# A two-block transformer kernel: the feed-forward down projections computed by one level of Strassen's scheme

## What is computed

```python
D_MODEL, SEQ, D_FF = 1024, 512, 2816
# first block
f = (jax.nn.silu(h @ ffn_w_gate[l]) * (h @ ffn_w_up[l])) @ ffn_w_down[l]
x = x + rmsnorm(f, post_ffn_norm[l])
# second block, layers 0 and 1
h = causal_dwconv_2(x @ w_up, conv_w)
g, v = jnp.split(h, 2, axis=-1)
f = (jax.nn.silu(g) * v) @ w_down
x = layer_norm(ALPHA * x + f, ln_g[layer, 1], ln_b[layer, 1])
```

## Time and profile before

| | |
|---|---|
| median of 3 runs | 1866.66 us (1864.05 to 1867.01) |
| span of the profiled execution | 1862.7 us |
| TensorE busy | 1826.8 us, 98% |
| VectorE, ScalarE, GpSimd busy | 928.4, 723.4, 342.4 us |
| down projections, first to last matmul | 553.28 to 674.50, 1208.72 to 1329.94, 1735.42 to 1854.88 us |

### The profile page before, as it was taken

How to read it: one execution, slowest core, us unless ns; L and a number is a source line. 1 busy time by engine, 2 the same in 40 slices (tenths; PEclk the granted TensorE clock), 3 DMA queues, 4 the chain that set the end, 5 groups by cost and what they waited for, 6 DMA issues and landing times.

```text
span 1862.7 us, 23259 instructions
## 1 busy us (share of the span) xinstructions
PE 1826.8 (98%) x9750; PEld 1527.4 (82%) x9750; DVE 928.4 (50%) x1455; ACT 723.4 (39%) x1221; POOL 342.4 (18%) x206
## 2 busy tenths in 40 slices
PE   7999988999999999999999999999999999999998
PEld 6788977888888888777788888888788898888886
DVE  5686644332232244785455555523574455555334
ACT  6664344322322243557634343321333243343211
POOL 1434533111110033321141111100201321111000
PEclk9999999999999999999999999999999999999999
DMA  5212032233223232110122223332332323222331
GB/s 198 74 57 69 8 125 81 91 110 119 99 100 104 87 135 92 68 46 24 46 78 103 91 91 98 118 113 80 113 103 80 112 91 109 95 91 94 122 102 68
DMA packets 29653, 171.53 MB, mean 92 GB/s; under 512 B 3378, under 2 KB 6490, under 8 KB 11754
## 3 DMA queue, kind: packets, MB, share of 16 engines
q1 hardware_dynamic: 29548, 170.03, 26.5%
HBM read 167.88 MB, written 3.68 MB: 92 GB/s over the span
## 4 chain that ended last, share of the span: by engine, by line
PE 94%; DVE 3%; ACT 1%; POOL 1%; DMA 0%; issue 0%; SPq 0%; ACTq 0%
PE ps L578 28%; PE ps L580 28%; PE ps L579 27%; PE ps L1116 2%; PE ps L1083 1%; PE ps L1079 1%; PE ps L1101 1%; POOL wL L2505 1%; PE ps L658 1%; PE ps L708 1%; PE ps L1047 1%; ACT wH L1287 1%; DVE hL L1825 1%; PE ps L862 0%; PE ps L871 0%; DMA x<-in_x 0%
## 5 line engine op out<-in xcount | busy, mean ns | idle before, releaser
L578 PE MATMUL ps<-hH,wH 128*128 128x512 f32 (+1 forms) x1568 | 594.9, 379 | 4.4 <-DVE rows L2240 1.5
L580 PE MATMUL ps<-hH,wL 128*128 128x512 f32 (+1 forms) x1568 | 590.0, 376 | 0.0
L579 PE MATMUL ps<-hL,wH 128*128 128x512 f32 (+1 forms) x1568 | 589.9, 376 | 0.0
L1818 DVE TENSOR_TENSOR wL<-raw,wH 128x1024 fp32r<-128x1024 f32 (+1 forms) x212 | 259.4, 1263 | 331.8 <-ACT wH L1287 331.8
L1287 ACT ACTIVATE wH<-raw 128x1024 fp32r<-128x1024 f32 (+2 forms) x298 | 290.3, 1023 | 273.6 <-PE ps L580 273.5
L578 PEld LDWEIGHTS ps<-hH,wH 128*128 128x128 f32 x1568 | 295.1, 188 | 59.3 <-DVE rows L2240 2.0
L580 PEld LDWEIGHTS ps<-hH,wL 128*128 128x128 f32 x1568 | 295.0, 188 | 54.3
L579 PEld LDWEIGHTS ps<-hL,wH 128*128 128x128 f32 x1568 | 295.2, 188 | 52.3
L2505 POOL TENSOR_TENSOR wL<-raw,wH 128x1024 fp32r<-128x1024 f32 (+2 forms) x86 | 205.0, 2406 | 670.2 <-ACT wH L1287 662.4
L578 PE MATMUL ps<-wH,aH 128*128 128x512 f32 x528 | 205.6, 389 | 0.0
L580 PE MATMUL ps<-wH,aL 128*128 128x512 f32 x528 | 205.4, 389 | 0.0
(11 more groups left out here) (367 smaller groups left out, 1845.5 us busy)
## 6 DMA issues: line engine op xcount, KB each, us to landing
raw<-in_wbig SPq DMA_DIRECT2D x139, 1024.0 KB, 4.8
rows<-in_rows SPq DMA_DIRECT2D x12, 512.0 KB, 6.0
x<-in_x SPq DMA_DIRECT2D x8, 512.0 KB, 5.7
raw<-in_wbig SPq DMA_DIRECT2D x8, 512.0 KB, 3.5
out<-x SPq DMA_DIRECT2D x4, 512.0 KB, 2.6
u_rows<-u_scratch SPq DMA_DIRECT2D x4, 384.0 KB
near<-u_rows SPq DMA_DIRECT2D x1, 1024.0 KB, 7.9
raw<-in_wbig SPq DMA_DIRECT2D x1, 1000.0 KB, 9.0
```

The source lines that it names most:

```text
L578: e.matmul(o, hi, m_hi, start=first, stop=False)
L579: e.matmul(o, hi, m_lo, start=False, stop=False)
L580: return e.matmul(o, lo, m_hi, start=False, stop=end)
L1818: e.tensor_tensor(wL[r][:, cs], raw[r][:, cs], wH[r][:, cs].bitcast(F32), ALU.subtract).then_inc(*low_dve.one(c, h))
```

## The change

Only the three down projections change, with what makes their inputs and takes their results. The product is cut in two along each axis: tokens (256 and 256), features (1408 and 1408, eleven k-tiles each) and columns (512 and 512). In place of eight block products there are seven, each with 11 k-tiles, two token tiles and three matmuls: 66 matmuls a product.

The core of the diff:

```diff
@@ -36,6 +36,11 @@
...
+    def blocks(name, layer):
+        plan.append((name, layer, "blocks", 11, 2048))
+        for _ in range(11):
+            plan.append((name, layer, "none", 0, 0))
...
@@ -413,12 +425,18 @@
...
         R = Region(BIG, TOP)
-        aH = R("aH", [128, 22, 512], F32R)
-        aL = R("aL", [128, 22, 512], F32R)
...
+        aR = R("aR", [128, 11, 1536])
...
+        ft = [R("ft", [128, 512]) for _ in range(4)]
+        agH = [R("agH", [128, 1024], F32R) for _ in range(2)]
+        agL = [R("agL", [128, 1024], F32R) for _ in range(2)]
+        extra0 = R("extra0", [128, 2048])
+        store0 = R("store0", [128, 512])
+        extra1 = at("extra1", FT, [128, 2048])
+        scaled_f = at("scaled_f", XRES + 16384, [128, 8, 512])
+        parts_f = at("parts_f", XRES + 32768, [128, 8, 512])
+        junk_f = aR[:, 0:4, 0:128]
+        raw_ring = [raw[1], raw[0], extra0, extra1]
...
@@ -560,7 +579,89 @@
...
+        def store(k):
+            return aR[:, k - 1, 512:1024] if k else store0[:, :]
...
+        def half_free(n, v):
+            if v < 4:
+                return dn.pe.at(n, "done", 9) if v < 2 else dn.pe.at(n, "P5", 1)
+            return dn.pe.at(n, "P4", 1) if v in (8, 9) else dn.pe.at(n, "done", 7 + v)
 
...
@@ -661,6 +762,83 @@
...
+            def down(n, turn_tile):
+                banks = {"P1": (4, 5), "P5": (2, 3), "P7": (0, 1), "P6": (6, 7), "P4": (4, 5), "P2": (6, 7), "P3": (0, 1)}
+                first = {"P1": (2, 0, "w01"), "P5": (0, 1, "w01"), "P7": (3, 2, "w2"), "P6": (1, 3, "w3")}
...
+                for q in range(11):
+                    r = (q + 1) % 2
+                    for p in ("P1", "P5", "P7", "P6") if q < 10 else ("P1", "P6", "P7", "P5"):
+                        a, b, ready = first[p]
+                        w.wait_ge(*dn.dve.at(n, "alo", q))
+                        w.wait_ge(*dn.dve.at(n, ready, q))
+                        for j in range(2):
+                            if q == 0:
+                                clear(banks[p][j])
+                            m = product(p, j, r, a, b, q == 0, q == 10)
+                            if q == 10:
+                                m.then_inc(*dn.pe.one(n, p, j))
+                    if q < 10:
+                        m.then_inc(*dn.pe.one(n, "done", q))
...
+                for v in range(4):
+                    ready_b(v)
+                    for kk in range(2):
+                        for j in range(2):
...
+                            m = part_b(v, "P4", kk, j, v == 0 and kk == 0, False)
+                    m.then_inc(*dn.pe.one(n, "done", 11 + v))
+                for j in range(2):
...
+                for v in range(6, 13):
+                    ready_b(v)
+                    for p in ("P2", "P3"):
...
+                            m = part_b(v, p, 0, j, v == 6, False)
+                    m.then_inc(*dn.pe.one(n, "done", 11 + v))
+                    if v == 9:
+                        turn_tile(2)
+                    if v == 11:
+                        turn_tile(3)
+                for j in range(2):
+                    for vs in ((13, 14), (15, 16)) if j == 0 else ((14, 15), (13, 16)):
+                        for p in ("P2", "P3"):
+                            for v in vs:
+                                ready_b(v)
+                                m = part_b(v, p, 0, j, False, v == 16)
...
@@ -1275,20 +1451,76 @@
...
+            def high_a(n, q):
+                r, src = (q + 1) % 2, raw_a(q)
+                w.wait_ge(*(dn.pe.at(n, "done", q - 2) if q > 1 else chunk_done(DOWN[n] - 2 + q)))
+                w.wait_ge(*dn.pool.at(n, "S1", q))
+                e.activation(agH[r][:, :], aR[:, q, 0:1024], ACT.Copy).then_inc(*dn.act.one(n, "ahi", q))
+                w.wait_ge(*landed_a(n, q))
+                w.wait_ge(*dn.pool.at(n, "T1", q))
+                e.activation(wH[r][:, 0:1024], src[:, 0:1024], ACT.Copy).then_inc(*dn.act.one(n, "w01", q))
+                w.wait_ge(*dn.dve.at(n, "T3", q))
+                e.activation(wH[r][:, 1024:1536], src[:, 1536:2048], ACT.Copy).then_inc(*dn.act.one(n, "w2", q))
+                w.wait_ge(*dn.pool.at(n, "T2", q))
+                e.activation(wH[r][:, 1536:2048], store(q), ACT.Copy).then_inc(*dn.act.one(n, "w3", q))
+            def high_b(n, v):
+                w.wait_ge(*half_free(n, v))
+                if v < 6:
+                    w.wait_ge(*dn.pool.at(n, "T4", B_KS[v][-1]))
+                else:
+                    w.wait_ge(*landed_b(n, B_KS[v][0]))
+                e.activation(w_view(wH, v), w_source(v), ACT.Copy).then_inc(*dn.act.one(n, "whi", v))
+                if v >= 6:
+                    w.wait_ge(*dn.pool.at(n, "S4", B_KS[v][0]))
+                e.activation(a_view(agH, v), a_source(v), ACT.Copy).then_inc(*dn.act.one(n, "bhi", v))
...
@@ -1798,18 +2025,98 @@
...
+            def third_sum(n, q):
+                src = raw_a(q)
+                w.wait_ge(*landed_a(n, q))
+                e.tensor_tensor(src[:, 1536:2048], src[:, 1536:2048], src[:, 512:1024], ALU.subtract).then_inc(*dn.dve.one(n, "T3", q))
+            def low_a(n, q):
+                r, src = (q + 1) % 2, raw_a(q)
+                w.wait_ge(*dn.act.at(n, "ahi", q))
+                e.tensor_tensor(agL[r][:, :], aR[:, q, 0:1024], agH[r][:, :].bitcast(F32), ALU.subtract).then_inc(*dn.dve.one(n, "alo", q))
+                for name, cs, part_of in (("w01", slice(0, 1024), src[:, 0:1024]), ("w2", slice(1024, 1536), src[:, 1536:2048]),
+                                          ("w3", slice(1536, 2048), store(q))):
+                    w.wait_ge(*dn.act.at(n, name, q))
+                    e.tensor_tensor(wL[r][:, cs], part_of, wH[r][:, cs].bitcast(F32), ALU.subtract).then_inc(*dn.dve.one(n, name, q))
+            def low_b(n, v):
+                w.wait_ge(*dn.act.at(n, "whi", v))
+                e.tensor_tensor(w_view(wL, v), w_source(v), w_view(wH, v).bitcast(F32), ALU.subtract).then_inc(*dn.dve.one(n, "wlo", v))
...
+            def down(n, turn_tile, add_last, finish):
+                for q in range(1, 11):
+                    if q < 10:
+                        third_sum(n, q + 1)
+                    low_a(n, q)
...
@@ -2483,13 +2832,88 @@
...
+            def branch_sums(n, c0):
+                for m in range(22):
+                    if m == 21:
+                        weight_sums(n, 0)
+                    k = m % 11
+                    w.wait_ge(*ffn.dve.at("a", c0 + m))
+                    if m < 11:
+                        e.tensor_tensor(aR[:, k, 768:1024], aR[:, k, 512:768], aR[:, k, 768:1024], ALU.subtract).then_inc(*dn.pool.one(n, "S3", k))
+                    else:
+                        w.wait_ge(*dn.pool.at(n, "S3", k))
+                        e.tensor_tensor(aR[:, k, 256:512], aR[:, k, 1280:1536], aR[:, k, 768:1024], ALU.subtract).then_inc(*dn.pool.one(n, "S2", k))
+                        w.wait_ge(*dn.pool.at(n, "S2", k))
+                        e.tensor_tensor(aR[:, k, 0:256], aR[:, k, 256:512], aR[:, k, 512:768], ALU.add).then_inc(*dn.pool.one(n, "S1", k))
+            def weight_sums(n, q):
+                src = raw_a(q)
+                w.wait_ge(*dn.dve.at(n, "T3", q))
+                if q:
+                    w.wait_ge(*dn.dve.at(n, "alo", q - 1))
+                e.tensor_tensor(store(q), src[:, 1536:2048], src[:, 0:512], ALU.add).then_inc(*dn.pool.one(n, "T2", q))
+                e.tensor_tensor(src[:, 512:1024], src[:, 512:1024], src[:, 0:512], ALU.subtract).then_inc(*dn.pool.one(n, "T1", q))
+            def fourth_sum(n, q):
+                w.wait_ge(*dn.dve.at(n, "w3", q))
+                w.wait_ge(*landed_a(n, q))
+                w.wait_ge(*dn.pool.at(n, "T2", q))
+                e.tensor_tensor(store(q), raw_a(q)[:, 1024:1536], store(q), ALU.subtract).then_inc(*dn.pool.one(n, "T4", q))
+            def low_b(n, v):
+                w.wait_ge(*dn.act.at(n, "bhi", v))
+                e.tensor_tensor(a_view(agL, v), a_source(v), a_view(agH, v).bitcast(F32), ALU.subtract).then_inc(*dn.pool.one(n, "alo", v))
+            def down(n):
+                for q in range(1, 11):
+                    weight_sums(n, q)
...
+                def outer_sum(ks):
+                    w.wait_ge(*dn.dve.at(n, "alo", ks[-1]))
+                    w.wait_ge(*dn.pool.at(n, "S1", ks[-1]))
+                    for k in ks:
+                        e.tensor_tensor(aR[:, k, 256:512], aR[:, k, 1024:1280], aR[:, k, 256:512], ALU.subtract).then_inc(*dn.pool.one(n, "S4", k))
+                def add_x(i):
+                    if n:
+                        w.wait_ge(*ffn.act.at("x", n - 1, i))
+                        w.wait_ge(*(dn.dve.at(n, "C22", i - 2) if i > 1 else dn.dve.at(n, "P5", i)))
+                        e.tensor_tensor(q8v(x[:, i, :]), q8v(x[:, i, :]), whole(parts_f, i), ALU.add).then_inc(*dn.pool.one(n, "x", i))
+                for v in range(3):
+                    low_b(n, v)
+                add_x(2)
```

(24 more changed lines are left out.)

460 lines of the change are left out of this document (340 added, 120 removed).

## The result

| | before | after |
|---|---|---|
| median | 1865.36 us (1863.99 to 1867.01, 4 runs) | 1941.95 us (1940.74 to 1947.45, 4 runs) |
| ratio, 95% interval | | 1.0419 (1.0403 to 1.0435) |
| span of the profiled execution | 1862.7 us | 1938.9 us |
| first to last matmul start, three stages | 121.2, 121.2, 119.5 us | 135.9, 147.4, 150.5 us |

The change costs 4.2%; the two medians are 76.6 us apart. The prediction was 1939.0 us. The page of after answers to the earlier trace rows: TensorE is busy for 10 us less and its share of the chain fell from 94% to 74%, with VectorE and GpSimd in its place.

A forecast was written before the change was run, and what follows sets the result against it. TensorE bounds the kernel before, DVE's and POOL's passes in turn the changed stages: +10.4, +25.1, +26.8, +4 behind, +6 missed turns, together +72.3 on 1862.7, plus 4.0: 1939.0 us. Range 1895 to 1968 (8 in 10); main case 1928 to 1965.

The forecast's parts named there:

- The step of 0.2267 us: Down projections: each matmul takes 0.2267 us, so 462 take 104.7 us.
- Turn-taking and its prices: Two-input passes exclude each other: DVE 0.54 (512) and 1.09 (1024), POOL 1.17 (512), 0.61 (256); 7.3 us a q.
- The whole stage: Each down projection: passes in turn sum to 123.4 us in the first, 132.6 in the later two.
- Start: From the up projection's end to the start of the passes' sum: 0.9 us in the first stage, 6.4 in later ones.
- a wait of TensorE for a load: Sign that the prediction is wrong; a load takes 4.8 us and has three q's of time.
- Behind the stages: After the first two down projections, the next chunk's weights are split late: some 2 us each, +4.
- Other signs: `alo` and `w01` means near 2 us; second and third stages lose more than twice what the first loses.
- The clock stays at 1.00: Expected sign: TensorE's idle in the down projections is too short to lower its granted clock.
- 1 (only the first phase bound, 1897): Down projections: passes bind only the first phase, later ones keep TensorE's pace; +30, 1897 us, chance 0.12.
- 2 (overlap): Down projections: DVE's and POOL's passes overlap after all, so the change is faster; 1841 us, chance 0.09.
- 3 (a clock that falls for whole phases, 2059): First phases: TensorE's clock falls and matmuls take twice 0.2267 us; about 2059 us, chance 0.03.
- 4 (whole durations, 1991): Down projections: turns cost whole recorded durations, +17 us each; 1991 us, chance 0.09 (shared with many missed turns).

The follow-up runs named there:

- e2: Changed kernel with the weight sums T1, T2 and T4 made by VectorE in place of GpSimd; 1897.05 us.
- e4: Changed kernel with the first down projection's load of q = 2 issued before SyncE waits for the last branch; 1938.99 us.
- e8: Version with all passes on VectorE (1887.54 us), plus the earlier load, another product order for q = 0 and later ScalarE square roots; 1872.69 us.
- e12: e11 with loads of chunks 53 and 103 ahead of constants, chunk 102 split earlier, its low halves on VectorE; 1856.36 us, 0.9951 of the kernel before.
- e10: Version of 1867.08 us (e8 with single passes moved), with the next chunk's low halves behind the first two stages made by VectorE; 1865.82 us.
- e11: e10 with additions to x and norm passes moved into VectorE's later idle time, last S4 to GpSimd, in the later two stages; 1866.26 us.
- e6: Changed kernel without GpSimd's four additions to x in each of the second and third down projections; 1922.24 us.
- e1: Changed kernel with the fourth weight sum, T4, left out in all three down projections; 1913.51 us.
- e7: e4 with GpSimd making T2 and T1 of q = 1 before it waits for the last branch; 1936.93 us.

## Why the prediction was right

**The step of 0.2267 us** stands: the matmuls start 0.2267 us apart wherever TensorE neither waits nor runs slow behind a wait.

**Turn-taking and its prices.** 7.37 us a q against 7.3. T4's price, by leaving it out, is 1.10 against 1.17. VectorE back to back is 0.60 and 1.14 against the 0.54 and 1.09 that I took from passes in turn. By these figures VectorE's five cost 0.3 us a q more than I had and GpSimd's three 0.2 less: that the sum is so near is in part luck, since the two errors cancel. GpSimd alone at 128 x 256 takes 0.73 us (S2 at 553.61), so 0.61 in turn was near. The Trainium skill (GPSIMD Engine Reference, "3.1 Elementwise — side-by-side cycle accounting") gives 1.96 as the ratio of the two engines for a two-input add. Here it is 1.87 by the durations alone (1.29 to 0.69) and 1.83 by what a pass costs (1.10 to 0.60), and that factor is what e2 gains in a q, 3 x 0.50 = 1.5 us: the same sum on VectorE costs about half as much time.

**The whole stage.** In the three stages TensorE begins q = 10 here, and needs 5.44 us for it (PE timeline of after):

```profile
629.27 0.47 PE L679 MATMUL ps<-wH,agH 128*128 128x512 f32 x1 [1.06 <-DVE wL L2049]
...
1305.58 0.47 PE L679 MATMUL ps<-wH,agH 128*128 128x512 f32 x1 [1.06 <-DVE wL L2049]
...
1860.30 0.47 PE L679 MATMUL ps<-wH,agH 128*128 128x512 f32 x1 [1.04 <-DVE wL L2049]
```

First phase and rest, first stage: forecast 79.7 and 52.1, measured 82.1 and 54.0. For the second 85.2 and 61.3, measured 85.1 and 62.6. For the third the same, measured 85.1 and 65.6. With the 2 us for missed turns in each, the second (148.5 against 147.7) and the rest of the first (54.1 against 54.0) are nearly exact.

**Start.** The first long wait: q = 1 begins 11.0 us into the first stage, forecast 8.5. The step missed two things. It counted T3 of q = 2 as a pass only, and the load stood on SyncE behind a wait for the last branch; e4 puts that at 2.1 us of the stage, of which q = 1 begins 1.0 us earlier. And for the first stage it has no term for ScalarE's `w01` between GpSimd's T1 and VectorE's: in e4 1.5 us lie there, from 562.09 to 563.55, and q = 1 begins 9.9 us in. (Its own terms, 0.9, 4.7 and 2.7, add up to 8.3, not 8.5.) In the later two it is 15.1 us, forecast 14.0. The prediction named a wait of TensorE for a load as a sign of being wrong. The wait at 563.60 is put down to VectorE's `wL`, but VectorE had stood 6.96 us for that load, so in the first stage the sign is there in part.

**Behind the stages** +3.2 and +1.8 against 2 each.

**Other signs.** VectorE's `alo` has a mean of 2.10 us in the first stage's first phase, as forecast, but `w01` is at 1.2 to 1.4: what grew instead are the 512-wide `w2` and `w3`, 1.55 to 1.77. The second stage lost 1.8 times what the first lost, not more than twice; the third did, 2.1 times. And near the end of the third ScalarE waits 3.76 us for the load of the last piece (until 1918.52), which SyncE issues only when VectorE has the low half of v = 13. TensorE waits 2.61 us at 1922.11 behind it. The forecast has no term for this either. In the third stage of e8 to e12 ScalarE has such a wait, too: 6.5 us up to e10, 3.8 to 3.9 in e11 and e12.

**The clock** was the step with a wrong statement. "The clock stays at 1.00" is not what the windows say (length, busy us by engine, then the granted clock):

```profile
552.00:634.00 82.00, 63.90 (x265) 50.00 (x264) 74.06 (x55) 35.72 (x46) 58.90 (x35) 0.96 0.45 161
634.00:689.00 55.00, 50.61 (x219) 40.21 (x217) 46.74 (x47) 33.56 (x54) 47.14 (x28) 0.97 0.22 76
```

Behind the long waits TensorE's steps are 0.43 us for seven to fourteen matmuls, at the lower of its two levels, 1.2 GHz: the granted clock is 0.58 from 560 to 564 us and 0.56 from 564 to 568, and 1.00 ahead of and behind them. In the PE timeline of after (the last but one row is the last slow one):

```profile
563.60 0.77 PE L679 MATMUL ps<-wH,agH 128*128 128x512 f32 x1 [5.36 <-DVE wL L2049]
564.16 0.63 PE L680 MATMUL ps<-wL,agH 128*128 128x512 f32 x1
564.59 0.63 PE L681 MATMUL ps<-wH,agL 128*128 128x512 f32 x1
...
567.15 0.57 PE L681 MATMUL ps<-wH,agL 128*128 128x512 f32 x1
567.55 0.40 PE L679 MATMUL ps<-wH,agH 128*128 128x512 f32 x1
```

Behind the waits of 1.7 us in each q they are not slow. All slow steps are 23.6 us in the three stages. Not all of it is lost: behind the wait at 563.60 the 2 us are made good by a q that then has no wait at all. The forecast, which has no such step, is only 3.9 us short in all. How much the rest costs I haven't measured apart. One comparison hints at it: in the third stage the changed kernel and e4, with the same code there, wait 34.2 and 34.5 us, but the slow steps are 11.2 and 7.8, and the stage is 3.0 us longer where they are more.

**Rivals.** 1 (only the first phase bound, 1897) falls by e6 and by the waits for `agL` in the later phases. 2 (overlap) falls by e1 and e2. 3 (a clock that falls for whole phases, 2059) didn't come, only its beginnings. 4 (whole durations, 1991) is refuted by 7.37 us a q, where it had 0.69 x 3 + 1.22 x 2 + 1.29 x 3 = 8.4.

**Right in the mechanism, a little short in the sum**: +72.3 forecast, +76.2 measured. The 3.9 us between them are 2.3 in the first stage (mostly its start), 2.2 in the third, within the scatter seen there, 1.0 behind the stages, and 0.9 and 0.6 the other way in the second stage and ahead of the first. The forecast's own range is off by its own terms, too: 1929 to 1968 us, not 1928 to 1965.

## What to carry to other kernels

An engine at 18% is no room for work if its passes exclude those of the busy one: add the passes of both up, at what each holds, and give the work to the engine that holds for less long, or put GpSimd's passes beside VectorE's passes out of PSUM or with one SBUF input. A scheme that saves matmuls pays only while the element-wise passes it adds stay under what it leaves of TensorE's time: here 462 steps are 104.7 us, and VectorE alone, from the last branch to the last low half of the second stage, took 110 us in e10 (1212.4 to 1322.5), 108.7 of them busy. When the stage is shorter and the time isn't, look at the first chunks behind it and at their loads.

## What the runs showed of the hardware

- The exclusion needs two SBUF inputs on VectorE's side only. GpSimd's copy, one input, 0.605 us alone, still costs VectorE 0.42 us.
- A VectorE pass with one SBUF input (statistics, 0.69 us) or with one in PSUM (0.60 us a step) runs beside GpSimd unhindered.
- GpSimd's copy of 128 x 512 takes 0.605 us, half of its subtraction (1.29).
- TensorE's slow steps follow every wait of over 4 us in the down stages, and not those of 1.7 in each q. Between them it was mixed: in the changed kernel waits of 2.7 us have them, in e7 one of 2.67 at 569.95 has none; waits of 1.8 to 2.0 us have none or six to eight. So I draw no bound.
